# Combining merged into the next layer's mixer, block by block, in a two-layer mixer and MoE trunk on Trainium2

## The chip, the cores and the metric

The kernel runs on the 8 cores of one Trainium2 chip (two dies, cores 0 to 3 and 4 to 7). Each core works alone on half a sequence of a batch of four. The metric is the device time of the slowest core in microseconds.

## What is computed

```python
for l in range(DEPTH):                      # 2 layers, D_MODEL 1024, x is (4, 4096, 1024)
    m = hybrid_mixer(x, ...)                # z = x @ w_in (1024 x 2048); four groups of 256 channels:
    x = layer_norm(ALPHA * x + m, ln1)      #   spatial gating in chunks of 128, Conformer conv (31 taps),
    f = grouped_moe(x, ...)                 #   pooling over 2/4/8/16, gated conv (3 taps);
    x = layer_norm(ALPHA * x + f, ln2)      #   RMS norm of each group, then @ w_o (1024 x 1024)

def grouped_moe(x, ...):                    # 16 experts in 4 groups, best group, top 2 in it
    for e in range(N_EXPERTS):
        h = silu(xt @ w_gate[e]) * (xt @ w_up[e])              # 1024 x 512 each
        y = y + dense_gates[:, e:e + 1] * (h @ w_down[e])      # 512 x 1024
```

## The kernel before

A core holds 17 tiles of 128 tokens (2048 tokens and a halo tile) as f32 in `s_xtok`. MBLOCKS cuts them into block 0 (the halo) and blocks 1 to 4 (512 tokens each).

**Mixer.** For a block, `G_section` computes the spatial gating, `CPS_section` the other three groups, `O0_section` the product with w_o added to `s_xtok`, `A_section` the LN and a turned bf16 copy in `s_xT`, `R_section` the router; its `scatter` calls send each token's bf16 row to its two slots in `xg` in HBM (384 slots for an expert). The 31-tap convolution runs on PE as 62 matmuls for a block, each with a 128 x 128 diagonal `s_dg` that ACT or POOL makes just before, from `s_identf` and a column of taps, in four rotating buffers. RMS and LN over channels sum squares by f32 matmuls with `s_ones`.

**Experts.** `x_load` fetches an expert's 384 rows from `xg`, `x_turn` turns them, `s_wbuf` holds two experts' weights, and each result tile goes to `yg` in HBM. `cast_expert` has earlier copied the f32 weights (6.3 MB for an expert) to bf16 in HBM (`ew`), in two halves, on POOL's queue, with two in flight; `load_expert` reads them from there on SP's queue.

**Combining.** For each tile two gathers fetch the rows of its two experts from `yg`, DVE multiplies them by `geff` (the gates) and adds them to `s_xtok`; then LN, scale and shift (`s_lnp`), and for layer 1's input the turned copy. All 17 tiles pass before layer 1's mixer starts in earnest; the last stage does the same for 16 tiles and writes the output.

**Order.** A planner, `arrange`, orders each program stretch (layer 0 up to its experts, combining with layer 1, the last combining) by the longest chain behind each instruction, with a cost for each kind. Within an engine the order is then fixed, DMA issues too: an instruction that waits holds all behind it. A branch for overfull experts stands after each layer's experts and isn't taken.

At the start SP loads constants, parameters and x, then zeroes `xg` from `s_scrb`; POOL loads w_in and w_o as bf16. Helper lines of the profile: L549 matmul, L558 activation, L562 two-tensor, L569/L571 tensor-scalar, L577 scalar-tensor-tensor, L585/L587 copies on ACT/DVE, L621 LN statistics, L653 and L1196 transposes, L372 plain DMA, L375 scatter, L380 gather.

## Time and profile before

| | us |
|---|---|
| Median of 3 runs (2164.21 to 2168.35) | 2166.95 |
| The profiled execution, its own time | 2165.37 |
| Its span on the slowest core (core 1) | 2164.3 |
| PE busy (matmuls), ACT, DVE, POOL | 1319.7, 778.4, 954.6, 559.4 |
| The 8 cores' spans | 2128.2 to 2164.3 |

The span is from the first to the last instruction of core 1; the execution's own time is the slowest core's device time. Busy times overlap and say nothing alone; the stages have different limits and are read one by one.

### The profile page before, as it was taken

To read this page: it belongs to the slowest core of one execution; us is meant where nothing else is said; L and a number is where in the kernel's file an instruction comes from. 1 tells how busy PE (TensorE), PEld (TensorE's weight loads), DVE (VectorE), ACT (ScalarE), POOL (GpSimd) and SP (SyncE) were. 2 spreads that over 40 slices of the span, in tenths; PEclk is the share of its full clock that TensorE was granted. 3 is DMA by queue.
4 is the path that set the end of the run, shared out by engine and by line. 5 is a ranking of instruction groups with operands and counts; after the bars stand their busy time and mean duration, and the time that the engine had idled before them with its cause. 6 is when DMAs were issued, how large, how long until landed. Compare 5 with 4: busy or idle time off the path is not lost.

```text
span 2164.3 us, 26021 instructions; the slowest of 8 cores (2128.2 to 2164.3 us)
## 1 busy us (share of the span) xinstructions
PE 1319.7 (61%) x7130; PEld 644.5 (30%) x7130; DVE 954.6 (44%) x2121; ACT 778.4 (36%) x1478; POOL 559.4 (26%) x595
## 2 busy tenths in 40 slices
PE   3202858667576399999113475676757379999500
PEld 2101313223232255554101222222223145555200
DVE  0101563736447123333568453563727413323498
ACT  3202626446263222222224543545445322222022
POOL 3000305061334200000546403325152400000285
PEclk9655979879797599999555697888878689999855
DMA  9994599999993279996982799999999559998474
GB/s 207 232 141 121 59 119 105 108 136 109 125 144 129 103 265 315 323 306 226 195 209 93 99 111 107 114 110 135 109 149 123 169 187 306 317 318 301 184 235 165
DMA packets 85690, 379.22 MB, mean 175 GB/s; under 512 B 10528, under 2 KB 19488, under 8 KB 69664
## 3 DMA queue, kind: packets, MB, share of 16 engines
q0 software_dynamic: 31440, 165.59, 52.9%
q1 hardware_dynamic: 54096, 211.84, 29.5%
q8 instruction: 65, 1.06, 0.2%
q14 instruction: 89, 0.73, 0.1%
HBM read 402.47 MB, written 189.27 MB: 273 GB/s over the span
## 4 chain that ended last, share of the span: by engine, by line
PE 34%; DMA 34%; DVE 10%; issue 10%; another core or an unknown queue 5%; ACT 4%; POOL 2%; SPq 0%; DVEq 0%; ACTq 0%; POOLq 0%
PE pb L549 31%; DMA ew<-exp_w 28%; DMA s_scr<-yg,s_gai 2%; DVE s_xtok L577 2%; PE pT L1196 2%; DMA xg<-s_scrb,s_sci 1%; POOL s_xtok L562 1%; DMA s_scr<-gmwT 1%; DVE s_xtok L562 1%; DVE s_sm L621 1%; ACT s_xT L585 1%; DVE s_sm L577 1%; POOL xg L375 1%; DVE s_scr L562 1%
## 5 line engine op out<-in xcount | busy, mean ns | idle before, releaser
L549 PE MATMUL pb<-s_xT,s_wbuf 128*128 128x384 bf16 (+2 forms) x2992 | 677.6, 347 | 142.0 <-ACT s_scr L585 54.1
L549 PEld LDWEIGHTS pb<-s_xT,s_wbuf 128*128 128x128 bf16 x2992 | 279.0, 101 | 386.9 <-issue 215.9
L562 POOL TENSOR_TENSOR s_xtok<-s_xtok,s_lnp 128x1024 f32<-128x1024 f32 x99 | 246.3, 2507 | 85.0 <-ACT s_sm L558 42.8
L549 PE MATMUL pb<-s_hbb,s_dg 128*128 128x512 bf16 (+1 forms) x558 | 176.2, 400 | 141.1 <-POOL s_dg L571 77.0
L585 ACT COPY s_xT<-pT 128x1024 bf16<-128x1024 bf16 x163 | 164.7, 1010 | 229.6 <-PE pT L1196 205.5
L380 POOL DMA_INDIRECT s_scr<-yg,s_gai x46 | 62.7, 1364 | 652.1 <-DMA yg<-s_yT 611.3
L549 PE MATMUL pb<-s_wbuf,s_scrb 128*128 128x512 bf16 x768 | 221.3, 378 | 12.1 <-DVE s_xT L587 5.2
L653 PE MATMUL pT<-s_identb,s_scrb 128*128 128x128 bf16 x536 | 94.6, 261 | 176.7 <-ACT s_scrb L558 81.0
L372 POOL DMA_DIRECT2D ew<-exp_w x64 | 34.7, 543 | 597.4 <-DMA ew<-exp_w 531.6
L549 PE MATMUL pb<-s_wbuf,s_yT 128*128 128x512 bf16 x528 | 155.8, 417 | 34.9 <-DVE s_yT L577 30.3
L558 ACT ACTIVATE s_scr<-pb 128x384 f32<-128x384 f32 (+2 forms) x148 | 72.2, 499 | 266.0 <-PE pb L549 143.1
L558 ACT ACT_TABLE_LOAD x65 | 83.4, 1283 | 224.4 <-DMA xg<-s_scrb 82.5
L1196 PE MATMUL pT<-s_identb,s_xT 128*128 128x128 bf16 x768 | 133.8, 227 | 46.1 <-DMA s_xT<-xg 39.9
L562 DVE TENSOR_TENSOR s_scrb<-s_scr,pb 128x384 bf16<-128x384 f32 x128 | 68.5, 551 | 204.1 <-PE pb L549 165.5
L558 ACT ACTIVATE s_dg<-s_identf,s_ppb 128x128 bf16<-128x128 f32 x279 | 105.8, 397 | 125.9 <-PE pb L549 100.6
L571 POOL TENSOR_SCALAR s_dg<-s_identf,s_ppb 128x128 bf16<-128x128 f32 x279 | 108.2, 391 | 164.4 <-PE pb L549 122.3
L549 PEld LDWEIGHTS pb<-s_hbb,s_dg 128*128 128x128 bf16 x558 | 56.9, 103 | 227.6 <-issue 210.0
L558 ACT ACTIVATE s_scr<-s_scr 128x512 f32<-128x512 f32 (+1 forms) x144 | 85.5, 594 | 91.8 <-PE pb L549 29.9
L653 PEld LDWEIGHTS pT<-s_identb,s_scrb 128*128 128x128 bf16 x536 | 52.9, 117 | 205.9 <-issue 197.8
L587 DVE COPY s_xT<-pb 128x512 f32<-128x512 f32 x96 | 61.8, 686 | 116.8 <-PE pb L549 110.9
L587 DVE COPY s_yT<-pb 128x512 f32<-128x512 f32 x96 | 62.5, 686 | 112.5 <-PE pb L549 112.5
L549 PE MATMUL pb<-s_wbuf,s_xT 128*128 128x512 bf16 x264 | 104.0, 429 | 13.3 <-DMA s_wbuf<-w_in 11.2
(105 smaller groups left out, 1727.4 us busy)
## 6 DMA issues: line engine op xcount, KB each, us to landing
ew<-exp_w POOLq DMA_DIRECT2D x64, 1536.0 KB
s_wbuf<-ew SPq DMA_DIRECT2D x96, 1024.0 KB, 10.9
s_xT<-xg SPq DMA_DIRECT2D x32, 768.0 KB, 8.1
yg<-s_xT SPq DMA_DIRECT2D x48, 512.0 KB, 8.1
yg<-s_yT SPq DMA_DIRECT2D x48, 512.0 KB, 9.5
xg<-s_scrb SPq DMA_DIRECT2D x1, 12288.0 KB, 136.5
s_xtok<-x SPq DMA_DIRECT2D x17, 512.0 KB, 23.2
out<-s_xtok SPq DMA_DIRECT2D x16, 512.0 KB, 2.7
```

The costliest lines, as they stand in the source:

```text
L372: self._dma(E, lambda e: e.dma_start(out=out, in_=in_), semkey, w, r, group_left, size)
L375: self._dma(self.pool, lambda e: e.indirect_dma_start(out=out, out_offset=bass.IndirectOffsetOnAxis(ap=idx, axis=0), in_=in_, in_offset=None),
L380: self._dma(self.pool, lambda e: e.indirect_dma_start(out=out, out_offset=None, in_=in_, in_offset=bass.IndirectOffsetOnAxis(ap=idx, axis=0)),
L549: em.op(PE, lambda e: e.matmul(out.ap, lhsT.ap, rhs.ap, start=start, stop=stop), w=[out], r=[lhsT, rhs])
L558: em.op(ACT, lambda e: e.activation(out=out.ap, in_=in_.ap, func=func, **kw), w=[out], r=rr, tab={AF.Ln: "ln", AF.Exp: "ln", AF.Silu: "sil ...
L562: em.op(E, lambda e: e.tensor_tensor(out=out.ap, in0=a.ap, in1=b.ap, op=op), w=[out], r=[a, b])
L571: em.op(E, lambda e: e.tensor_scalar(out=out.ap, in0=a.ap, scalar1=a1, scalar2=a2, op0=op0, op1=op1), w=[out], r=rr)
L577: em.op(E, lambda e: e.scalar_tensor_tensor(out=out.ap, in0=a.ap, scalar=sv, in1=b.ap, op0=op0, op1=op1), w=[out], r=rr)
L585: em.op(E, lambda e: e.copy(out=out.ap, in_=in_.ap), w=[out], r=[in_])
L587: em.op(E, lambda e: e.tensor_copy(out=out.ap, in_=in_.ap), w=[out], r=[in_])
L653: em.op(PE, lambda e, kc=kc: e.transpose(out=pT(kc * 128, (kc + 1) * 128).ap, in_=xb(kc * 128, (kc + 1) * 128).ap, identity=identb().ap), ...
L1196: em.op(PE, lambda e_, src=src, dst=dst: e_.transpose(out=dst.ap, in_=src.ap, identity=identb().ap), w=[dst], r=[src, identb()])
```

## The change

Nine groups of edits, made together:

- Gates travel with the rows: `xg` rows are 1056 bf16 wide, with the f32 gate behind the 1024 values; the expert stage multiplies its output by the gate where DVE had copied it (half on DVE, half on ACT).
- Gathers add into `s_xtok` (`gather_add`); for a dropped token the index points to a zero row of `yg`. `C_section` (LN, scale, turned copy) takes the combining's place in layer 1's block loop, ahead of `G_section` of the same block.
- The 62 diagonals are made once a layer into `s_dgm`, by four POOL instructions in `load_layer_params`; layer 1's are made at the end of layer 0's mixer.
- Squares of two channel halves are added first, so one f32 matmul with `s_ones` stands where two stood.
- Only experts 0, 1 and the even ones (PRE) are cast to `ew`; 3, 5, ... 15 are loaded by POOL from the f32 weights into `s_wbuf`.
- Copies may run on ACT or DVE (AD) and sums on DVE or POOL (VP); the planner picks. Its DMA rate is 270 in place of 300 and its sizes for POOL's transfers are larger.
- At the start, `xg` is zeroed from `s_gov` in two halves of each row, after block 2's x tiles; blocks 3 and 4 of x come after it, casts after those. The identity arrives as bf16.
- `s_xT` (all blocks) and `s_yT` become one buffer `s_xy` with two blocks and yT; scratch shrinks.
- `dynamic_dma_scratch_size` is 4096 in place of 8192.

```diff
+PRE = [e for e in range(NE) if e % 2 == 0 or e == 1]
...
+        VP, AD = (DVE, POOL), (ACT, DVE)
...
+    def gather_add(self, out, in_, idx, semkey, w=(), r=(), group_left=0):
         self._dma(self.pool, lambda e: e.indirect_dma_start(
-            out=out, out_offset=None, in_=in_, in_offset=bass.IndirectOffsetOnAxis(ap=idx, axis=0)),
-            semkey, w, r, group_left)
...
             def sD(r, i):
-                tt(POOL, xtile(i), xtile(i), lnp(goff, goff + D), ALU.mult)
-                tt(POOL, xtile(i), xtile(i), lnp(goff + D, goff + 2 * D), ALU.add)
+                tt(VP, xtile(i), xtile(i), lnp(goff, goff + D), ALU.mult)
+                tt(VP, xtile(i), xtile(i), lnp(goff + D, goff + 2 * D), ALU.add)
...
         def rms_group(yf, nb, gcol, c0):
-            sq = S(TM0 + 2, 0, nb)
-            for j in range(2):
-                act(sq, yf[j], AF.Square)
-                mm(B[4](0, nb), ones(), sq, j == 0, j == 1)
+            sq, sq1 = S(TM0 + 2, 0, nb), S(TM0 + 1, 0, nb)
+            act(sq, yf[0], AF.Square)
+            act(sq1, yf[1], AF.Square)
+            vt(sq, sq, sq1, ALU.add)
+            mm(B[4](0, nb), ones(), sq, True, True)
             ve = S(TM0 + 1, 0, nb)
             ts(DVE, ve, B[4](0, nb), 1.0 / 256.0, ALU.mult, RMS_EPS, ALU.add)
             powm(ve, ve, nb)
...
+            for q in range(0, 62, 16):
+                m = min(16, 62 - q)
+                dst = dgm(q * 128, (q + m) * 128).v(lambda ap: ap.rearrange("p (k c) -> p k c", c=128))
+                idv = identb().v(lambda ap: ap.rearrange("p (o c) -> p o c", o=1).to_broadcast([128, m, 128]))
+                wv_ = ppb(PP_DW + q, PP_DW + q + m).v(
+                    lambda ap: ap.rearrange("p (k o) -> p k o", o=1).to_broadcast([128, m, 128]))
+                tt(POOL, dst, idv, wv_, ALU.mult)
...
+            if tag or e not in PRE:
+                for q in range(3):
+                    em.dma(POOL, wbuf(base + q * 4096, base + (q + 1) * 4096).ap, ew_d[l, e, :, q * 4096:(q + 1) * 4096],
+                           "dw%sp%d%s" % ("gud"[q], s, tag), w=[wbuf(base + q * 4096, base + (q + 1) * 4096)])
+                return
...
-        for b_ in range(2, len(MBLOCKS)):
-            x_in(b_, [wbuf(16384, 24576)])
-        em.dma(SP, xgD.ap[0:NSLOT, :].rearrange("(j p) d -> p j d", p=128),
-               scrb(0, D).ap.rearrange("p (o d) -> p o d", o=1).to_broadcast([128, NSLOT // 128, D]), "dz",
-               w=[xgD.rows(0, 1000)], r=[scrb(0, D), xtile(NT - 1)])
...
+        x_in(2, [wbuf(16384, 24576)])
+        for h in range(2):
+            em.dma(SP, xgD.ap[0:NSLOT, h * GW // 4:(h + 1) * GW // 4].rearrange("(j p) d -> p j d", p=128),
+                   gov(0, GW // 4).ap.rearrange("p (o d) -> p o d", o=1).to_broadcast([128, NSLOT // 128, GW // 4]), "dz",
+                   w=[xgD.rows(1000 * h, 1000 * h + 1000)], r=[gov(), xtile(8)], group_left=1 - h, size=NSLOT * GW)
+        x_in(3, [xgD.rows(0, 2000)])
+        x_in(4, [xgD.rows(0, 2000)])
+        for l in range(L):
...
+        for e in PRE:
+            cast_expert(0, e, [gtok.rows(NT - 1, NT)])
...
+        def c_gather(k, i, yg):
+            c = k * NT + i
+            em.gather_add(xtile(i).ap, yg.ap, gai(c, c + 1).ap, "dg%d" % (i + NT * k), w=[xtile(i), gtok.rows(i, i + 1)],
+                          r=[yg.rows(0, NSLOT + 1), gai(c, c + 1), xtile(i)])
...
-                            slot = dgi[0] % 4
-                            dgi[0] += 1
-                            wcol = ppb(PP_DW + j * 31 + k, PP_DW + j * 31 + k + 1)
-                            GE = (POOL, ACT, POOL, ACT)[slot]
-                            if GE is ACT:
-                                act(dg(slot * 128, (slot + 1) * 128), identf(), AF.Identity, scale=wcol)
-                            elif GE is DVE:
-                                ts(GE, dg(slot * 128, (slot + 1) * 128), identf(), wcol, ALU.mult)
-                            else:
-                                ts(GE, dg(slot * 128, (slot + 1) * 128), identf(), wcol, ALU.mult, 0.0, ALU.add)
-                            mm(pcs[j](0, nb), dg(slot * 128, (slot + 1) * 128), hbs[j](k, k + nb), k == 0, k == 30)
+                            q = (j * 31 + k) * 128
+                            mm(pcs[j](0, nb), dgm(q, q + 128), hbs[j](k, k + nb), k == 0, k == 30)
...
+                for k in range(2):
+                    xr, xf = xrow[b == nblk - 1], xrowf[b == nblk - 1]
+                    gcol = xf(0, nt * GW // 2).v(lambda ap: ap.rearrange("p (t c) -> p t c", t=nt)[:, :, D // 2:D // 2 + 1])
+                    gcol.box = xr[0](D, GW).box[:3] + (xr[nt - 1](D, GW).box[3],)
+                    cpy(DVE, gcol, ge.v(lambda ap: ap[:, k * nt:(k + 1) * nt].rearrange("p (t o) -> p t o", o=1)))
...
+                        em.scatter(xgD.ap, sci(c, c + 1).ap, xf(t * GW // 2, (t + 1) * GW // 2).ap, "dsc%d" % k,
+                                   w=[xgD.rows(c, c + 1), xgD.rows(1000 + c, 1001 + c)],
+                                   r=[xr[t](0, GW), sci(c, c + 1)], group_left=nt - 1 - t, size=128 * GW * 2)
...
+            def C_section(b):
+                t0, nb = MBLOCKS[b]
+                tiles = list(range(t0 // 128, (t0 + nb) // 128))
+                pipeline(tiles, ln_stages(2048) + xT_stages(scale0=hflag(), pt_fixed=0, rows=xbx))
+
+            if l > 0:
+                for (t0, nb) in MBLOCKS:
+                    for k in range(2):
+                        for i in range(t0 // 128, (t0 + nb) // 128):
+                            c_gather(k, i, ygD[l - 1])
+                for e_ in PRE:
+                    cast_expert(l, e_, [gtok.rows(NT - 1, NT)])
+            enter = X_section if l == 0 else C_section
+            enter(0)
             if skip0:
                 CPS_section(0)
             fb = 1 if skip0 else 0
+            if fb:
...
+                    enter(b + 1)
+                    G_section(b + 1)
+                    CPS_section(b + 1)
+                A_section(b)
+                R_section(b)
...
+            if not last:
+                load_layer_params(l + 1)
...
-                        cpy(DVE, yb(nh * 512, (nh + 1) * 512), pY())
+                        gate = gsl(s * CT + j, s * CT + j + 1)
+                        if nh == 0:
+                            ts(DVE, yb(nh * 512, (nh + 1) * 512), pY(), gate, ALU.mult)
+                        else:
+                            act(yb(nh * 512, (nh + 1) * 512), pY(), AF.Identity, scale=gate)
...
+        for g0 in range(1, NT, 4):
+            for k in range(2):
+                for i in range(g0, g0 + 4):
+                    c_gather(k, i, yg)
+        pipeline(list(range(1, NT)), ln_stages(2048) + [c_out])
```

The order of instructions at three places. First the start. SP before, from its first x tile to the first loads of cast weights:

```order
L372 DMA s_xtok<-x 128x1024
L372 DMA s_trash<-trash 128x34
L372 DMA s_ppb<-pp 128x86
L372 DMA s_bc<-bc 128x768
L372 DMA s_lnp<-lnp 128x2048
L372 DMA s_scr<-gmwT 128x512
L372 DMA s_xtok<-x 128x1024 x16
L372 DMA xg<-s_scrb 128x48x1024
L372 DMA s_wbuf<-ew 128x4096 x6
```

The same in the change:

```order
L402 DMA s_ebase<-ebase 128x16
L402 DMA s_trash<-trash 128x34
L402 DMA s_lnp<-lnp 128x2048
L402 DMA s_xtok<-x 128x1024 x4
L402 DMA xg<-s_gov 128x48x264 x2
L402 DMA s_xtok<-x 128x1024 x8
L402 DMA yg<-s_gov 4x1x256 x2
L402 DMA s_wbuf<-ew 128x4096 x4
L402 DMA s_ppb<-pp 128x86
```

The zeroing stood behind all 17 x tiles; now it stands behind nine, is in two parts and reads `s_gov`. DVE in the change, around its first write of `s_gov` (the router of block 0; `s_xtok<-s_xtok,pb` is the output sum of block 1's tiles):

```order
L629 COPY s_xy<-pT 128x8x128
L614 SCALAR_TENSOR_TENSOR s_scrb<-s_gtmp,s_sm,s_bc 128x256
L614 SCALAR_TENSOR_TENSOR s_xy<-s_scr,s_ppb 128x512 x2
L633 COPY s_scrb<-s_rb 128x1
L599 TENSOR_TENSOR s_gov<-s_rb 128x16
L614 SCALAR_TENSOR_TENSOR s_xtok<-s_xtok,pb 128x512 x2
L665 BN_STATS s_sm<-s_xtok 128x6 x2
L667 BN_AGGR s_sm<-s_sm 128x2
```

The write stands behind block 1's mixer and ahead of block 1's output sums. ACT before, around its first write into the part of `s_scrb` that the zeroing reads (the two `s_scrb<-s_scr,s_ppb 128x128`, of block 0's convolution):

```order
L558 ACTIVATE s_sm<-s_sm 128x1 x4
L585 COPY s_yT<-pT 128x256
L585 CAST s_scrb<-s_xtok 128x1024 x4
L585 COPY s_xT<-pT 128x8x128 x2
L558 ACTIVATE s_scrb<-s_scr,s_ppb 128x128 x2
L585 CAST s_scrb<-s_xtok 128x1024
L585 COPY s_scr<-pb 128x128
L585 COPY s_xT<-pT 128x8x128
L558 ACTIVATE s_scr<-s_scr 128x128
```

That write had the turned copies of block 1 around it. Second, POOL at the end of layer 0's mixer, before (`xg<-s_scrb,s_sci` are scatters):

```order
L571 TENSOR_SCALAR s_dg<-s_identf,s_ppb 128x128 x17
L372 DMA ew<-exp_w 48x16384
L375 DMA xg<-s_scrb,s_sci 10496x1024 x8
L562 TENSOR_TENSOR s_xtok<-s_xtok,s_lnp 128x1024 x8
L375 DMA xg<-s_scrb,s_sci 10496x1024 x8
L1243 TENSOR_LOAD s_flag
```

and in the change:

```order
L599 TENSOR_TENSOR s_xtok<-s_xtok,s_lnp 128x1024 x7
L405 DMA xg<-s_scrb,s_sci 10496x528 x4
L599 TENSOR_TENSOR s_dgm<-s_identb,s_ppb 128x2048
L405 DMA xg<-s_scrb,s_sci 10496x528 x4
L599 TENSOR_TENSOR s_dgm<-s_identb,s_ppb 128x2048
L405 DMA xg<-s_scr,s_sci 10496x528 x4
L599 TENSOR_TENSOR s_dgm<-s_identb,s_ppb 128x2048
L405 DMA xg<-s_scr,s_sci 10496x528 x4
L599 TENSOR_TENSOR s_dgm<-s_identb,s_ppb 128x1792
L402 DMA s_wbuf<-exp_w 128x4096 x21
L1318 TENSOR_LOAD s_flag
```

Layer 1's diagonals now stand between the scatters, and 21 loads of f32 expert weights follow. Third, POOL behind the branch, where combining begins, before:

```order
L380 DMA s_scr<-yg,s_gai 128x1024 x4
L380 DMA s_yT<-yg,s_gai 128x1024 x2
L372 DMA s_wbuf<-w_in 128x8x512
L380 DMA s_scr<-yg,s_gai 128x1024
L372 DMA s_wbuf<-w_in 128x8x256
L372 DMA s_wbuf<-w_in 128x8x768
L380 DMA s_scr<-yg,s_gai 128x1024
L372 DMA s_pwb<-cf_pw 128x2x256
L380 DMA s_scr<-yg,s_gai 128x1024
L372 DMA s_wbuf<-w_in 128x8x512
L380 DMA s_scr<-yg,s_gai 128x1024
L380 DMA s_yT<-yg,s_gai 128x1024
```

and in the change:

```order
L410 DMA s_xtok<-yg,s_gai 128x1024 x4
L402 DMA s_wbuf<-w_in 128x8x512
L410 DMA s_xtok<-yg,s_gai 128x1024 x3
L402 DMA s_wbuf<-w_in 128x8x256
L410 DMA s_xtok<-yg,s_gai 128x1024
L402 DMA s_wbuf<-w_in 128x8x768
L410 DMA s_xtok<-yg,s_gai 128x1024
L402 DMA s_wbuf<-w_in 128x8x512
L410 DMA s_xtok<-yg,s_gai 128x1024 x4
L402 DMA s_wbuf<-w_o 128x4x1024 x2
L410 DMA s_xtok<-yg,s_gai 128x1024 x9
L599 TENSOR_TENSOR s_xtok<-s_xtok,s_lnp 128x1024 x5
```

The gathers write `s_xtok` itself and stand nearly all ahead of the first pass with `s_lnp`.

## Rows read from the trace of the kernel before

**Rows 1.** The page: the span of the profiled execution.

```profile
span 2164.3 us, 26021 instructions; the slowest of 8 cores (2128.2 to 2164.3 us)
```

**Rows 2.** Stretches of core 1 by stage; under its header line.

```profile
core 1: us, PE busy (x) PEld busy (x) DVE busy (x) ACT busy (x) POOL busy (x), PEclk, DMA share, GB/s
0.00:205.00 205.00, 38.40 (x232) 23.99 (x232) 11.71 (x44) 43.02 (x88) 24.05 (x51) 0.67 0.94 185
205.00:735.00 530.00, 350.55 (x1617) 147.85 (x1617) 275.04 (x779) 258.99 (x527) 174.91 (x217) 0.83 0.80 111
735.00:1040.00 305.00, 283.05 (x1792) 157.50 (x1792) 94.87 (x164) 75.52 (x112) 0.00 (x0) 0.97 0.80 270
1040.00:1190.00 150.00, 32.83 (x173) 18.00 (x174) 104.79 (x145) 48.47 (x85) 89.77 (x56) 0.53 0.69 165
1190.00:1740.00 550.00, 332.59 (x1526) 139.97 (x1524) 265.59 (x703) 249.22 (x506) 181.82 (x224) 0.80 0.92 123
1740.00:2040.00 300.00, 282.29 (x1792) 157.13 (x1792) 94.47 (x160) 75.72 (x112) 0.00 (x0) 0.98 0.82 274
2040.00:2164.00 124.00, 0.00 (x0) 0.00 (x0) 108.10 (x128) 27.50 (x49) 88.83 (x48) 0.50 0.60 204
```

**Rows 3.** Waits from 0 to 210 us: waiter, awaited, us, times, longest.

```profile
ACT L558 <- DMA xg<-s_scrb: 82.5, 1, 82.5
```

**Rows 4.** DMA issues from 0 to 210 us: count, size, median us to landing.

```profile
xg<-s_scrb SPq DMA_DIRECT2D x1, 12288.0 KB, 136.5
```

**Rows 5.** Timeline of PE, start and length in us, at 93 us.

```profile
93.08 3.57 PE L549 MATMUL pb<-s_wbuf,s_xT 128*128 128x512 bf16 x8 [11.16 <-DMA s_wbuf<-w_in]
```

**Rows 6.** Groups of instructions, 205 to 735 us (layer 0 mixer).

```profile
L549 PE MATMUL pb<-s_hbb,s_dg 128*128 128x512 bf16 x248 | 80.7, 406 | 47.6 <-POOL s_dg L571 34.1 <-ACT s_dg L558 9.9 <-DVE s_hbb L577 1.4
L562 POOL TENSOR_TENSOR s_xtok<-s_xtok,s_lnp 128x1024 f32<-128x1024 f32 x34 | 79.6, 2359 | 28.1 <-ACT s_sm L558 25.1 <-ACT s_xtok L558 3.0
...
L549 PE MATMUL pb<-s_scr,s_ones 128*128 128x512 f32 (+1 forms) x88 | 47.5, 638 | 12.0 <-ACT s_scr L558 4.2 <-DVE s_rb L562 2.9 <-ACT s_sm L558 2.4
...
L558 ACT ACTIVATE s_dg<-s_identf,s_ppb 128x128 bf16<-128x128 f32 x122 | 45.8, 396 | 46.9 <-PE pb L549 44.8 <-PE pT L653 1.0
...
L558 ACT ACTIVATE s_xtok<-s_xtok,s_sm 128x1024 f32<-128x1024 f32 x17 | 20.9, 1236 | 16.3 <-DVE s_sm L577 16.3
```

**Rows 7.** The same, PE, 1190 to 1740 us (layer 1 mixer).

```profile
L549 PE MATMUL pb<-s_hbb,s_dg 128*128 128x512 bf16 x248 | 82.5, 427 | 83.0 <-POOL s_dg L571 40.5 <-ACT s_dg L558 19.8 <-DVE s_hbb L577 15.3
...
L549 PE MATMUL pb<-s_scr,s_ones 128*128 128x512 f32 x80 | 41.6, 616 | 10.4 <-ACT s_scr L558 4.7 <-ACT s_sm L558 3.7 <-DVE s_scr L562 1.5
```

**Rows 8.** Waits of POOL, 200 to 720 us.

```profile
POOL ew L372 <- DMA ew<-exp_w: 181.2, 19, 15.3
```

**Rows 9.** Waits of POOL, 1190 to 1700 us.

```profile
POOL ew L372 <- DMA ew<-exp_w: 258.2, 25, 21.8
```

**Rows 10.** DMA from 400 to 560 us (casts of expert weights).

```profile
DMA packets 1342, 19.10 MB, mean 119 GB/s; under 512 B 304, under 2 KB 304, under 8 KB 816
...
ew<-exp_w POOLq DMA_DIRECT2D x11, 1536.0 KB
```

**Rows 11.** DMA from 800 to 900 us (experts of layer 0).

```profile
DMA packets 7420, 31.93 MB, mean 319 GB/s; under 512 B 662, under 2 KB 662, under 8 KB 5294
...
q1 hardware_dynamic: 7412, 31.82, 97.2%
```

**Rows 12.** DMA rate in 40 slices of 1690 to 1740 us.

```profile
GB/s 426 416 426 423 439 410 357 321 233 105 16 0 13 0 0 0 177 308 341 13 0 0 0 0 0 0 0 0 0 0 39 210 213 213 213 216 213 213 148 20
```

**Rows 13.** DMA from 1040 to 1100 us (combining and weight loads).

```profile
DMA packets 7193, 12.44 MB, mean 207 GB/s; under 512 B 597, under 2 KB 4949, under 8 KB 7189
...
s_scr<-yg,s_gai POOLq DMA_INDIRECT x12, 21.2
```

**Rows 14.** Groups of instructions, 2040 to 2164 us.

```profile
L562 DVE TENSOR_TENSOR s_xtok<-s_xtok,s_lnp 128x1024 f32<-128x1024 f32 x16 | 37.5, 2345 | 5.3 <-POOL s_xtok L562 5.2
...
L380 POOL DMA_INDIRECT s_scr<-yg,s_gai x22 | 30.2, 1371 | 314.4 <-DMA yg<-s_yT 304.9 <-DVE s_sm L621 6.3 <-issue 2.5
```

396 lines of the change are left out of this document (198 added, 198 removed).

## The prediction

> **What bounds the kernel now.** I cut the span into stages first. The page gives the span, 2164.3 us, and the profiled execution's own time is 2165.4 us, which is 1.6 us under the median of the runs, 2166.95; I make the sum against 2165.4. [Rows 1, 2] Seven stretches tell different stories. Read per stretch how much of it PE, DVE, ACT and POOL fill, then the DMA share.
>
> From 0 to 205 us PE works 38 us. The list of waits names one event: ACT stands 82.5 us behind the DMA that zeroes xg, because ACT's next write goes into s_scrb, which that DMA reads. [Rows 3] The DMA takes 136.5 us. [Rows 4] Before it, PE waited for w_in until 93 us. [Rows 5]
>
> In the mixers (205 to 735, 1190 to 1740) no engine is full: PE 350 of 530 and 333 of 550 us, ACT and DVE about half. [Rows 2] The stages are chains over engines. Two groups stand out: the convolution's matmuls idle 47.6 us, 44.0 of it for their diagonals; in layer 1 they idle 83.0, 60.3 for them. [Rows 6, 7] POOL, which makes half of the diagonals, itself stands in its queue behind the casts of expert weights for 181 and 258 us. [Rows 8, 9]
>
> In the expert stages PE is nearly full, 283 of 305 and 282 of 300 us, and DMA is 97% busy as well. [Rows 2, 11] From 1040 to 1190 and 2040 to 2164 PE does next to nothing: this is the combining, run by DMA, DVE and POOL. [Rows 2]
>
> **The change part by part.**
>
> *Start.* The zeroing now reads s_gov and stands after five x tiles plus block 2's four; twelve of 17 x tiles come after the weights. Read side before the first full block: weights 12.6 MB in f32, five tiles 2.6, parameters and small tables 3.2, in all 18.4 MB. At 0.32 MB/us (below) that is 58 us, where PE had waited until 93 [rows 5]. From there to 205 us the kernel needed 112 us, 82.5 of them the stall [rows 3], so about 30: the state of 205 us is reached at 88 us at best, at 122.5 if only the stall goes. I take 100: **-105 us**. Where the stall goes: DVE's first write of s_gov must wait for the zeroing, and POOL's first scatter too. What is queued behind it is block 1's output sums, for which PE's output banks wait. The zeroing (13.0 MB in rows of 1056 bytes, half the old row) starts near 65 us and takes 41 us at 0.32, or 82 if the short rows cost double; it is over by 106 to 147. The s_gov write stands behind block 1's whole mixer, so near 150. I price the wait at nothing; cover gone, it is a rival. Casts start only after the last x tile, some 130 to 170 us. 18 halves at 160/11 = 14.5 us [rows 10] are 261 us, over by about 430, before the first expert. Hidden.
>
> *Mixer of layer 0 (530 us).* Diagonals are made once per layer, four POOL instructions of 2048 columns (by POOL's 2.36 us for 1024 [rows 6] 4.7 us each, 19 us, under the weight load). The 44.0 us of waits go, and ACT loses 45.8 us of work [rows 6], POOL about as much. The matmuls with s_ones in f32 halve: 47.5 / 2 = 24 us of PE [rows 6]. POOL's queue waits for fewer casts; its 181 us [rows 8] were mostly idle anyway, and I credit 15 us, for the LN passes and scatters behind them (bounds 0 and the 136 us that PE idles beside the diagonals). **-83 us**, to about 447. Copies that may go to ACT or DVE and sums that may go to DVE or POOL only smooth this; I credit nothing. The end of the mixer now has the next layer's diagonals between POOL's scatters: one instruction of 4.7 us stands ahead of the last four scatters. Small, inside my rounding.
>
> *Combining into the mixer (150 + 550 us).* Gates now multiply at the expert's output, where DVE copied anyway; half of these go to ACT, which is 75 of 305 us busy [rows 2]. Nothing. The 34 gathers add into s_xtok. Only block 0's and 1's ten gathers (5.2 MB) and w_in (8.4 MB read) stand before the mixer's first full block: 13.6 MB, 42 us at 0.325. If the adding reads and writes SBUF at a cost like a second transfer, ten times 1.6 us more, 58. I take 50, plus 30 for LN, turning and the first matmuls: 80 where 150 stood, -70. The mixer then loses 60.3 and 41.6 / 2 = 21 [rows 7], and gains the LN and turning of blocks 2 to 4: 12 tiles by some 3.3 us on ACT (the LN pass takes 1.24 [rows 6], and cast and copy are of its size), 40 us on an engine with 300 us free, and two passes of s_lnp each. I charge 16 us: -65. Together **-135 us**.
>
> The passes with s_lnp may now run on DVE. Beside POOL, DVE's takes 2.35 us for 1024 columns, as long as POOL's own in the mixer, so two passes at once gain nothing and I credit nothing for the free choice. [Rows 6, 14] The Trainium skill (SBUF — State Buffer, on the port pair that DVE and GpSimd share) says that a DVE instruction with two SBUF inputs and a GpSimd instruction that reads SBUF shut each other out for their whole length. The 2.35 us agrees; were the rule wrong, the passes of blocks 2 to 4 would halve and the sum be some 25 us less.
>
> *Experts.* Seven of 16 (3, 5, ... 15) are no longer cast to HBM and read back; POOL loads them as f32 into s_wbuf. For a pair of experts the HBM side moves 3.15 (cast one) + 6.29 (direct) + 1.58 (rows in) + 3.15 (rows out) = 14.2 MB, against 11.0. A pair has 35.7 us (305 and 300 us for 16 with their ends, of which 285 are matmuls). DMA is 97.2% busy at 319 GB/s already [rows 11]. What rate can it reach? Short bursts show 410 to 439 [rows 12]. Longest mixed stretches: the casts read 211 and write 105 GB/s (19.10 MB less 2.1 of eight scatters, over 160 us), with scatters 330 in all [rows 10]; 1040 to 1100 us wrote 12.44 MB and read 18.7 (the 6.3 MB of weights are f32 at the source), 312 GB/s [rows 13]. I take 325, the figure between, and nearest to the 319 of the stage itself: 14.2 / 0.325 = 43.5 us for a pair, 7.8 over PE's, by seven pairs 55 us for a layer, **+110 us** for two. Lower bound: at the bursts' 426, 33 us, hidden, 0. Upper: the direct load reads at the casts' 211 GB/s, 29.8 us in place of 7.4 (3.15 at 426) in the pair's 34.7: 57.1, +150 for a layer, +300. PE then waits for s_wbuf where today it waits for nothing.
>
> *Last stage (124 us).* DVE loses two sums of the gathers for a tile. It was DVE's and POOL's stage [rows 2]; now 32 gathers (16.8 MB) and the output (8.4 MB) are 77 us at 0.325, plus 18 for first landing and last tile: 95. POOL has 32 x 1.37 us of issues [rows 14] and some 15 passes, 79, under that. If adding doubles a gather, 147. I take 110: **-14 us**.
>
> Sum: 2165.4 - 105 - 83 - 135 + 110 - 14 = **1938 us**; about 1940 as a median.
>
> **Rivals.**
> 1. *Expert loads stay hidden.* For it: bursts of 426. Against: 97.2% busy at 319. 1938 - 110 = 1828 us. Chance 0.12.
> 2. *The memory side holds a middle rate*, half way between the casts' 330 and the lowest long burst, 410 [rows 10, 12]: 370 GB/s, 38.4 us for a pair, +19 for a layer instead of +55: 1866 us. For it: neither row is the mix to come. Against: no stretch of 50 us or more shows it. 0.12.
> The Trainium skill (HBM Reference, the bandwidth table) gives a core about 358 GB/s when both cores of a stack stream; by that alone a pair takes 39.5 us and the whole 1882. No stage here reaches it; the casts' 330 is nearest.
> 3. *Direct loads run at the casts' rate.* Same kind of transfer, though those write to HBM. 1938 + 190 = 2128 us. 0.10.
> 4. *Adding in the DMA costs a second transfer.* No row shows it. +8 at layer 1's start, +37 at the end: 1983 us. 0.13.
> 5. *The mixers don't get shorter* because dependent steps, not diagonals, set them, with smaller scratch and shared ports: the change doesn't do what it says. 83 + 65 back: 2086 us. For it: half-idle engines. Against: 104 us of waits by name [rows 6, 7]. 0.09.
> 6. *The zeroing is waited for again*, at s_gov, if it takes its 136 us from 65 on: DVE held until 200, +50: 1988 us. 0.07.
> 7. *Slower.* One mechanism: the f32 loads of seven experts starve PE. It decides when it costs 110 + 227 = 337 us, 24 for a pair, that is, when one direct load takes over 32.5 us; the casts' rate gives 29.8, so it needs them a tenth worse than anything here. 2200 us. 0.05.
> The forecast itself, within 45 us: 0.32.
>
> **The numbers.** The range 1825 to 2090 takes in cases 1, 2, 4, 5 and 6 and leaves out 3 and 7 and the far sides of the rest. Faster by over 0.2% (about what a measurement of this kernel can tell from no change) 0.93, the same 0.01, slower 0.06: every case but 7 ends below.
>
> **What would show it.** No 82 us wait of ACT near 100 us; block 1 underway at 100. No waits for diagonals; f32 matmuls with s_ones halved; experts of layer 0 starting near 550 us. Expert stages of some 355 us with PE waiting for s_wbuf from exp_w. Gathers landing at 6 us (one transfer) or 8 and more (two). The last stage at 110 us. Most fragile is the rate of the direct loads; next, how much of the mixers' idle time follows the diagonals.

## The result, and the profile after

The changed kernel takes 2118.99 us (median of 4 runs, 2117.39 to 2122.18) beside 2167.65 us for the kernel before on the same chip: ratio 0.978, 95% interval 0.9763 to 0.9797. I had forecast 1940 us, a gain of 225; 49 came, and the time lies above my range of 1825 to 2090. In some executions of these kernels one die or both ran at a lower granted clock and took longer (with eleven experts cast, below, 2056.62 us with four cores at 0.77 to 0.78, beside 2008.49 with all at 0.81 to 0.83); ratios and their intervals leave such executions out, the medians given do not.

The page's span, then the changed kernel's stretches under their header line, cut at the first read of rows of `xg`, the first gather, and, for layer 1, PE's first matmul of a full block.

```profile
span 2117.7 us, 23728 instructions; the slowest of 8 cores (2092.0 to 2117.7 us)
...
core 3: us, PE busy (x) PEld busy (x) DVE busy (x) ACT busy (x) POOL busy (x), PEclk, DMA share, GB/s
0.00:95.00 95.00, 33.15 (x240) 23.37 (x241) 24.48 (x81) 21.40 (x43) 23.83 (x22) 0.91 1.00 208
95.00:588.00 493.00, 321.63 (x1560) 140.44 (x1558) 325.19 (x837) 193.66 (x347) 145.20 (x106) 0.82 0.62 117
588.00:992.00 404.00, 311.73 (x1792) 162.53 (x1792) 96.34 (x172) 75.73 (x124) 12.58 (x22) 0.91 0.78 204
992.00:1100.00 108.00, 14.41 (x123) 11.14 (x124) 22.18 (x47) 22.12 (x39) 74.19 (x46) 0.53 1.06 198
1100.00:1605.00 505.00, 331.07 (x1535) 142.28 (x1533) 345.35 (x841) 202.60 (x365) 156.64 (x108) 0.79 0.44 94
1605.00:1995.00 390.00, 306.51 (x1792) 162.00 (x1792) 95.61 (x164) 75.30 (x124) 11.20 (x21) 0.92 0.79 211
1995.00:2118.00 123.00, 0.00 (x0) 0.00 (x0) 64.81 (x97) 27.04 (x49) 90.65 (x47) 0.50 0.88 205
```

Against [rows 2], by my own terms. In layer 1, PE's first matmul that streams the 512 tokens of a block (`pb<-s_xT,s_wbuf` 128x512 before, `pb<-s_xy,s_wbuf` after) stands 127 us behind the first gather before and 107 after, and the rest of that mixer fell from 571 to 506. The two traces' timelines give these; before, matmuls of single tiles begin already 74 us behind the first gather, after, at the same 107.

| term | forecast | came |
|---|---|---|
| start (state of 205 us reached) | -105 | -110 |
| mixer of layer 0 (530 to 493) | -83 | -38 |
| layer 1, first gather to first full block (127 to 107) | -70 | -20 |
| layer 1, the rest (571 to 506) | -65 | -65 |
| experts, layer 0 (305 to 404) and 1 (303 to 390) | +55, +55 | +99, +87 |
| last stage (123 to 123) | -14 | 0 |
| sum | -227 | -47 |

Two terms came as worked out. The experts are the largest miss, 76 us; the start of layer 1 (50) and the mixer of layer 0 (45) are the next, then the last stage (14).

The groups that answer to [rows 6, 14]: the convolution and ones matmuls, POOL's passes with `s_lnp` in the mixer of layer 0; then gathers and passes of the last stage.

```profile
L599 POOL TENSOR_TENSOR s_xtok<-s_xtok,s_lnp 128x1024 f32<-128x1024 f32 x27 | 65.8, 2437 | 78.4 <-ACT s_xtok L595 65.5 <-DVE s_xtok L599 6.4 <-DVE s_rb L599 5.0
L586 PE MATMUL pb<-s_hbb,s_dgm 128*128 128x512 bf16 x248 | 54.8, 379 | 0.8 <-DVE s_scrb L633 0.7
...
L586 PE MATMUL pb<-s_scr,s_ones 128*128 128x512 f32 x40 | 27.6, 779 | 12.4 <-POOL s_scr L624 10.6 <-DVE s_rb L599 1.9
...
L410 POOL DMA_INDIRECT s_xtok<-yg,s_gai x32 | 54.4, 1700 | 58.9 <-DMA yg<-s_scr 51.0 <-issue 7.5 <-DMA s_xtok<-yg,s_gai 0.3
L599 POOL TENSOR_TENSOR s_xtok<-s_xtok,s_lnp 128x1024 f32<-128x1024 f32 x15 | 39.1, 2603 | 18.8 <-ACT s_sm L595 15.4 <-ACT s_xtok L595 2.7
L599 DVE TENSOR_TENSOR s_xtok<-s_xtok,s_lnp 128x1024 f32<-128x1024 f32 x17 | 29.0, 1707 | 15.0 <-POOL s_xtok L599 7.8 <-ACT s_xtok L595 6.5 <-ACT s_sm L595 0.3
```

The 47.6 us of idle time at the convolution are 0.8, and the ones matmuls fell by 20 us. Yet the mixer lost only 38: as a reader of a profile I would count 67 us gone by name.

PE's and ACT's waits in the experts of layer 0, 610 to 980 us, and one row of ACT's timeline there:

```profile
PE pb L586 <- ACT s_scr L595: 22.0, 25, 2.6
PE pb L586 <- DMA s_wbuf<-exp_w: 19.9, 7, 4.0
PE pT L1264 <- DMA s_xy<-xg: 12.7, 3, 11.4
...
ACT s_scr L595 <- DMA yg<-s_scr: 53.0, 11, 11.4
...
760.41 0.97 ACT L595 ACTIVATE s_scr<-pb 128x384 f32<-128x384 f32 x2 [8.62 <-DMA yg<-s_scr]
```

The 128x384 activation is the silu, not the output; all eleven of these waits of ACT stand before such a one. Why should a silu wait until an output tile has been written to HBM? Because of where its buffer lies. The silu goes to `SG(k, CAP)`, `s_scr` columns 542 k to 542 k + 384; the output buffers now lie in `s_scr` from 768 on, where before they had `s_xT` and `s_yT`. The second silu buffer, 542 to 926, overlaps the first output buffer.

Layer 1's start, ACT's timeline and then POOL's:

```profile
1058.82 1.04 ACT L631 CAST s_scr<-s_xtok 128x1024 bf16<-128x1024 f32 x1 [26.64 <-POOL s_xtok L599]
...
1036.58 1.68 POOL L410 DMA_INDIRECT s_xtok<-yg,s_gai  x1 [0.27 <-issue]
...
1052.33 1.55 POOL L410 DMA_INDIRECT s_xtok<-yg,s_gai  x1 [0.27 <-issue]
1053.32 7.72 POOL L599 TENSOR_TENSOR s_xtok<-s_xtok,s_lnp 128x1024 f32<-128x1024 f32 x3
...
1075.67 1.55 POOL L410 DMA_INDIRECT s_xtok<-yg,s_gai  x1
...
1091.25 2.95 POOL L599 TENSOR_TENSOR s_xtok<-s_xtok,s_lnp 128x1024 f32<-128x1024 f32 x1
```

POOL's passes for the first blocks stand behind two rows of gathers of later blocks, 1036 to 1053 and 1075 to 1091 us. ACT and PE wait for these passes: the turned copies of block 1 can't be made before them.

### The profile page after: what moved, and what is told of

It is laid out like the page before. It is cut to its first block, busy times and chain, and to the rows that moved or that the text cites. A ratio compares the mean times of both kernels' runs of the same rounds, so it can differ in the third digit from the quotient of the medians.

```text
span 2117.7 us, 23728 instructions; the slowest of 8 cores (2092.0 to 2117.7 us)
## 1 busy us (share of the span) xinstructions
PE 1318.5 (62%) x7040; PEld 641.8 (30%) x7040; DVE 974.0 (46%) x2238; ACT 617.9 (29%) x1089; POOL 514.3 (24%) x370
## 3 DMA queue, kind: packets, MB, share of 16 engines
q1 hardware_dynamic: 54080, 168.23, 23.7%
## 4 chain that ended last, share of the span: by engine, by line
PE 36%; DMA 20%; issue 17%; DVE 15%; POOL 6%; ACT 5%; DVEq 0%; another core or an unknown queue 0%; ACTq 0%; SPq 0%; POOLq 0%
PE pb L586 34%; DMA yg<-s_scr 13%; DMA s_xy<-xg 4%; POOL s_xtok L410 3%; ACT s_scr L595 2%; DMA s_xtok<-yg,s_gai 2%; DVE s_scr L599 2%; DVE s_rb L599 1%; POOL s_xtok L599 1%; PE pT L1264 1%; DVE s_scrb L614 1%; ACT L595 1%; DVE s_sm L614 1%; DVE s_sm L665 1%; DVE s_scr L606 1%
## 5 line engine op out<-in xcount | busy, mean ns | idle before, releaser
L586 PE MATMUL pb<-s_xy,s_wbuf 128*128 128x384 bf16 (+2 forms) x2992 | 741.9, 364 | 206.1 <-ACT s_scr L595 66.9
L586 PEld LDWEIGHTS pb<-s_xy,s_wbuf 128*128 128x128 bf16 x2992 | 289.8, 104 | 510.5 <-issue 349.1
L586 PE MATMUL pb<-s_wbuf,s_xy 128*128 128x512 bf16 x792 | 247.9, 423 | 13.5 <-DVE s_xtok L614 5.0
L1264 PE MATMUL pT<-s_identb,s_xy 128*128 128x128 bf16 x768 | 117.4, 234 | 87.2 <-DMA s_xy<-xg 79.0
L629 DVE COPY s_xy<-pT 128x1024 bf16<-128x1024 bf16 (+1 forms) x124 | 80.7, 651 | 148.2 <-PE pb L586 53.8
L410 POOL DMA_INDIRECT s_xtok<-yg,s_gai x66 | 109.5, 1660 | 122.2 <-DMA yg<-s_scr 102.3
L586 PE MATMUL pb<-s_hbb,s_dgm 128*128 128x512 bf16 (+1 forms) x558 | 116.5, 370 | 26.8 <-POOL s_dgm L599 22.9
L586 PEld LDWEIGHTS pb<-s_wbuf,s_xy 128*128 128x128 bf16 x792 | 81.6, 106 | 126.1 <-issue 65.0
L665 DVE BATCH_NORM_STATS2 s_sm<-s_xtok 128x6 f32<-128x512 f32 x132 | 85.9, 681 | 62.3 <-DMA s_xtok<-yg,s_gai 61.2
L595 ACT ACTIVATE s_xtok<-s_xtok,s_sm 128x1024 f32<-128x1024 f32 x66 | 81.3, 1238 | 79.8 <-DVE s_sm L614 67.5
```

Of the source, the lines that this page charges most:

```text
L410: self._dma(self.pool, lambda e: e.indirect_dma_start(out=out, out_offset=None, in_=in_, in_offset=bass.IndirectOffsetOnAxis(ap=idx, axis= ...
L586: em.op(PE, lambda e: e.matmul(out.ap, lhsT.ap, rhs.ap, start=start, stop=stop), w=[out], r=[lhsT, rhs])
L595: em.op(ACT, lambda e: e.activation(out=out.ap, in_=in_.ap, func=func, **kw), w=[out], r=rr, tab={AF.Ln: "ln", AF.Exp: "ln", AF.Silu: "sil ...
L629: em.op(E, lambda e: (e.copy if e is ACT.e else e.tensor_copy)(out=out.ap, in_=in_.ap), w=[out], r=[in_])
L665: em.op(DVE, lambda e, c=c: e.bn_stats(out=SMT(i, c * 6, c * 6 + 6).ap, in_=xtile(i, c * 512, (c + 1) * 512).ap), w=[SMT(i, c * 6, c * 6 + ...
L1264: em.op(PE, lambda e_, src=src, dst=dst: e_.transpose(out=dst.ap, in_=src.ap, identity=identb().ap), w=[dst], r=[src, identb()])
```

## The experiments

Ratios are to the kernel before on the same chip, with 95% intervals; stages are of the profiled execution's slowest core, "start" being layer 0's first read of rows. The changed kernel: 0.978, start 588, experts 404 and 390. Where the experts load directly, their stage is not the same on all cores of one execution: in the changed kernel layer 0's takes 389 to 404 us on the eight cores, 398 at the mean, and layer 1's 390 to 397. So 10 us in the expert stage of one core say little, and I give the mean of the eight where it matters.

**What the direct loads cost alone.** In the kernel before, seven experts of a layer are loaded directly and no longer cast; the rest of its work stays. The branch that does it:

```diff
+            if not tag and e not in PRE:
+                for q in range(3):
+                    em.dma(POOL, wbuf(...).ap, ew_d[l, e, :, q * 4096:(q + 1) * 4096], ...)
+                return
```

> The kernel before with one part of the change: experts 3, 5, ... 15 loaded directly as f32 by POOL, nine cast. Theory A: expert stages from 305 and 300 us to 390 to 410 us each, here too; the mixers, whose POOL queue stood 181 and 258 us behind the casts, shorten by 15 to 40 us each: total 2270 to 2330 us. Rival B (output path): expert stages stay near 305 us, total 2090 to 2150 us.

2204.02 us, 1.0115 (1.0091 to 1.014). Experts take 356 and 362 us, +51 and +59. The DMA of 710 to 1040 us:

```profile
DMA packets 17794, 77.82 MB, mean 236 GB/s; under 512 B 1575, under 2 KB 1575, under 8 KB 12394
...
q1 hardware_dynamic: 14746, 55.49, 49.3%
q0 software_dynamic: 3024, 22.02, 43.5%
```

The software queue's 22.02 MB are bf16 on arrival and twice that at the source: 99.8 MB in 330 us, 303 GB/s. My term of +55 a layer was right. The mixers meanwhile gained, from fewer casts alone: the start is at 698 and not 736, and from the first gather to layer 1's experts it takes 671 us and not 698. The stretch of layer 0's mixer, to set beside 530 us in [rows 2], and POOL's waits for casts, 200 to 690 us, beside 181.2 in [rows 8]:

```profile
205.00:698.00 493.00, 345.69 (x1620) 146.37 (x1618) 273.65 (x781) 259.53 (x530) 168.56 (x203) 0.85 0.46 75
...
POOL ew L373 <- DMA ew<-exp_w: 93.2, 9, 15.2
```

This is the length that the changed kernel's mixer has, 493 us, with the diagonals still made just before use. In the kernel before, the chain that ended last runs through the casts' transfers for 42.1% of layer 0's mixer and 70.9% of layer 1's; here it is 3.7% of layer 0's.

**The overlap of silu and output buffers.**

```diff
-                    sg = SG(fc % 2, CAP)
+                    sg = scr((fc % 2) * CAP, (fc % 2 + 1) * CAP)
```

> The changed kernel with one line other: the silu buffers of the expert stage at columns 0 and 384 of s_scr, not 0 and 542, so that the second (542 to 926) no longer overlaps the first output buffer (768 to 1792). Theory C (this overlap makes the silu of every other chunk wait until an output tile has landed in HBM, and the output tile wait for the silu's readers): the waits of ACT for yg, 53 us in 610 to 980 us, go; an expert takes 21.5 us as in the kernel before with direct loads, instead of 24.7; both expert stages shorten by 40 to 50 us; total 2020 to 2050 us. Rival A alone (only the direct loads' bytes hold the stage): same time, 2110 to 2125 us.

2066.27 us, 0.9473 (0.9445 to 0.9502): a one-line edit gains three points, more than the whole change had gained. Experts 371 and 369. ACT's and PE's waits, 610 to 950 us:

```profile
ACT s_scr L595 <- DMA yg<-s_scr: 31.7, 4, 15.8
...
PE pb L586 <- DMA s_wbuf<-ew: 19.7, 3, 12.5
PE pb L586 <- DVE s_xy L629: 9.2, 8, 1.7
PE pb L586 <- ACT s_scr L595: 8.5, 9, 1.9
```

PE now waits for weights, as I had expected of the change. ACT's four waits left are those of output tiles. At the mean of the eight cores the stages fell from 398 and 393 us to 366 and 365.

**The gates at the expert's output**, all on DVE, none on ACT.

```diff
-                        if nh == 0:
+                        if True:
                             ts(DVE, yb(nh ...
```

> The changed kernel with the gate of both output halves applied by DVE, none by ACT. Theory D (the ACT half of the output delays the silus queued behind it): expert stages shorten by 20 to 40 us each, 2040 to 2080 us. Theory C (overlap of buffers, whoever writes): within 15 us of the changed kernel, 2105 to 2135 us, the stall only sits on DVE instead.

2144.26 us, 0.9827 (0.9797 to 0.9857), experts 419 and 408. From 610 to 980 us ACT still waited 62.2 us for output writes, each time with a silu. So ACT's share of the gates was not the cause.

**Adding in the gathers.** The second row then replaces, and nothing is summed.

```diff
-            out=out, out_offset=None, in_=in_, in_offset=bass.IndirectOffsetOnAxis(ap=idx, axis=0),
-            compute_op=ALU.add), semkey, w, r, group_left)
+            out=out, out_offset=None, in_=in_, in_offset=bass.IndirectOffsetOnAxis(ap=idx, axis=0)),
+            semkey, w, r, group_left)
```

> The changed kernel with gathers that overwrite the rows of s_xtok instead of adding to them (the sum of the residual and the two experts is left out; all else is the same). If adding costs a second transfer, the landing of a gather falls by 1.5 us and more, the last stage from 112 to about 75 us and the combining of layer 0 by 20 to 40 us: 2040 to 2065 us. If adding is free: the same time as the changed kernel, 2110 to 2125 us.

2096.08 us, 0.9615 (0.9586 to 0.9644). From first gather to layer 1's experts 591 us, not 613; last stage 106, not 123. The last stage's gathers and DMA, without the adding:

```profile
L410 POOL DMA_INDIRECT s_xtok<-yg,s_gai x32 | 33.2, 1037 | 56.8 <-DMA yg<-s_scr 47.9 <-issue 7.6 <-DMA s_xtok<-yg,s_gai 0.9
...
q0 software_dynamic: 4608, 16.78, 49.1%
```

and with it, in the changed kernel:

```profile
q0 software_dynamic: 4608, 16.78, 70.0%
```

For the same 16.78 MB, adding holds the DMA engines for 70.0% of 123 us, 86, in place of 49.1% of 105, 52: 1.7 times as long. POOL's issue is 1.70 us in place of 1.04. The two places where it adds are 22 and 17 us shorter without. The slowest core's span fell by only 20, since its experts took 411 and 399; at the mean of the eight cores they take 398 and 396, as in the changed kernel, and the span falls by 32. This core is one with long expert stages.

**The second gate**, that is copied into the rows before their second scatter, left out (both scatters carry the first).

```diff
-                    cpy(DVE, gcol, ge.v(
+                    if k == 0:
+                      cpy(DVE, gcol, ge.v(
```

> The changed kernel without writing the gate of the second expert into the rows (those rows travel with the first expert's gate; the output is wrong by that). If the second set of scatters waits for the first to land because the gate column is rewritten (7.4 us at the end of layer 0's mixer, and within the blocks), each mixer's end shortens by 5 to 10 us: 2100 to 2112 us. If it is hidden: 2115 to 2122 us.

2110.32 us, 0.9664 (0.9602 to 0.9726); start at 577. That is 11 us in layer 0's mixer, at whose end, in the changed kernel, the second scatters wait 7.4 us for the first to land. From the first gather to layer 1's experts it is 603 us, 10 fewer, or 589 in place of 607 at the mean of the cores. So this copy costs 10 to 20 us in each mixer, a term that my sum did not have.

**The start alone.** In the kernel before, only the source of the zeroing was moved, to columns of `s_xT` that are free then.

```diff
-               scrb(0, D).ap.rearrange("p (o d) -> p o d", o=1)
+               zs.ap.rearrange("p (o d) -> p o d", o=1)
```

> The kernel before, with the rows that zero xg read from a stretch of s_xT that is free at that time; nothing else is changed. My sum priced ACT's stall of 82.5 us and the order of loads together at -105. If the stall alone is worth its length, the first mixer ends about 80 us sooner (experts of layer 0 at 655 us where they start at 736) and the time is 2085 to 2095. If another wait takes its place (the casts end at 629, the first scatter waits for the zeroing, the weights come late), less: 2110 to 2165.

2115.38 us, 0.9719 (0.968 to 0.9759): this alone gains at least as much as the whole change (2.8 points and 2.2). Start at 678, 58 sooner. POOL's waits, 200 to 670 us, show what stands now where the other 24 of the 82.5 us may have gone:

```profile
POOL xg L375 <- DMA xg<-s_xT: 62.9, 1, 62.9
```

The first scatter now waits for the zeroing, which takes 144.2 us beside seven casts. In the changed kernel no cast runs beside it: its two parts are issued at 76 us and have landed at 121, and nothing waits for them.

**Do waits for diagonals hold the mixers?** From both sides: sixteen buffers in the kernel before (with the DMA scratch at 4096, as in the changed one), and diagonals made again for each block in the changed one.

```diff
-        dg = sb("dg", 4 * 128, BF16)
+        dg = sb("dg", 16 * 128, BF16)
```

> The kernel before with sixteen buffers for diagonals in place of four. My sum took the convolution's waits for diagonals, 44.0 us in layer 0's mixer and 60.3 in layer 1's, as time on the path: most of it goes here, and the time falls by 60 to 100 us (2075 to 2115). If these waits lie beside other chains, as keeping the diagonals showed in the changed kernel, the waits shrink and the time stays within 10 us.

2162.16 us, 0.9923 (0.9898 to 0.9948). The waits fell less than I expected; the convolution's matmuls in the two mixers:

```profile
L549 PE MATMUL pb<-s_hbb,s_dg 128*128 128x512 bf16 x242 | 60.3, 396 | 40.0 <-POOL s_dg L571 37.0 <-DVE s_sm L577 2.3 <-DVE s_hbb L577 0.5
...
L549 PE MATMUL pb<-s_hbb,s_dg 128*128 128x512 bf16 x240 | 66.5, 431 | 63.3 <-POOL s_dg L571 22.3 <-ACT s_dg L558 20.8 <-DVE s_hbb L577 19.5
```

27 us of idle time went against [rows 6, 7], 22 of them waits for diagonals, and 17 us of the time (0.77%): more than the 10 of the one theory, far less than the 60 to 100 of the other. The busy time of these matmuls fell too, by 36 us, as they now stand closer together (six and eight of 248 are missing from the records). So some 60 us went from these rows and 17 from the kernel.

```diff
-            for q in range(0, 62, 16):
-                ...
-                tt(POOL, dst, idv, wv_, ALU.mult)
...
+                            if slot % 2:
+                                act(dgm(q, q + 128), identb(), AF.Identity, scale=wcol)
+                            else:
+                                ts(POOL, dgm(q, q + 128), identb(), wcol, ALU.mult, 0.0, ALU.add)
```

> The changed kernel with the diagonals made for each block by ACT and POOL in four rotating slots, as before the change, all else the same. If keeping the diagonals is worth what its waits and matmuls show (47 + 26 us in layer 0, 80 + 25 us in layer 1), the time rises by 100 to 180 us, 2220 to 2300 us. If the mixers are set by DVE's and the block chain's other steps, it rises by under 60 us, 2120 to 2180 us.

2118.85 us, 0.9714 (0.9678 to 0.975). ACT works 43 us more from 95 to 660 us; from 130 to 580 PE idles 10.8 us before the convolution's matmuls, 5.0 of it for POOL's diagonals; and the start is at 584. Kept diagonals are worth nothing in this kernel.

**Does PE hold the mixers?** Silu buffers apart, and 23 of the convolution's 31 taps left out.

```diff
-                    for k in range(31):
+                    for k in range(8):
```

> The changed kernel, silu buffers apart, with eight of the convolution's 31 taps (23 are left out). PE loses 4 blocks x 46 matmuls x 0.379 = 70 us of a mixer, and block 0's. If PE's row of work holds the mixer, each gets 60 to 75 us shorter and the time is near 1930. If steps over DVE, ACT and POOL hold it, each gets shorter by less than 30: 2010 to 2060.

2018.85 us, 0.9292 (0.9255 to 0.9329); start 573, layer 1's gathers to experts 586 where it was 605 with all taps. From 95 to 573 us:

```profile
95.00:573.00 478.00, 279.69 (x1337) 121.36 (x1360) 323.75 (x843) 189.19 (x345) 139.58 (x101) 0.78 0.73 121
```

With all taps PE was busy 325.02 us from 95 to 588. It lost over 40 us of work, though at a granted clock of 0.78 in place of 0.81, and the mixer lost 15. PE does not hold it.

**Does DVE, by the free choice of engines?** Every free copy on ACT, every free sum on POOL.

```diff
-        VP, AD = (DVE, POOL), (ACT, DVE)
+        VP, AD = POOL, ACT
```

> The changed kernel, with every copy that may run on ACT or DVE put on ACT, and every sum that may run on DVE or POOL put on POOL, as before. If DVE's added work (330 us busy of 502 in the first mixer, where it had 275 of 530) is what holds the mixers, they get shorter by 15 to 40 us each and the time falls to 2040 to 2090. If the free choice does what it is for, the time rises, by 10 to 60 us. If the chain is one of dependent steps on any engine, it stays within 10 us of the changed kernel.

2184.92 us, 1.0056 (1.0025 to 1.0086), all that the change had gained is gone: the free choice, which I priced at nothing, is worth some 60 us. Start 599 (+11), gathers to layer 1's experts 628 (+15), last stage 137 (+14), experts 413 and 402 (+9, +12). DVE is busy 296.87 us in the first mixer in place of 325.19, and the mixer is longer, so my suspicion of DVE's added work falls. The last stage shows what the choice saves there. On fixed engines, its stretch, its groups (2042 to 2178 us), and one row of DVE's and of POOL's timeline:

```profile
2042.00:2178.00 136.00, 0.00 (x0) 0.00 (x0) 66.50 (x80) 27.56 (x49) 123.80 (x64) 0.50 0.84 185
...
L599 POOL TENSOR_TENSOR s_xtok<-s_xtok,s_lnp 128x1024 f32<-128x1024 f32 x32 | 81.8, 2819 | 3.1 <-ACT s_xtok L595 3.1
...
L614 DVE SCALAR_TENSOR_TENSOR s_sm<-s_sm 128x1 f32<-128x1 f32 x16 | 40.4, 2523 | 11.8 <-ACT s_sm L595 11.8
...
2157.39 5.50 DVE L614 SCALAR_TENSOR_TENSOR s_sm<-s_sm 128x1 f32<-128x1 f32 x1 [0.69 <-ACT s_sm L595]
...
2155.35 7.51 POOL L599 TENSOR_TENSOR s_xtok<-s_xtok,s_lnp 128x1024 f32<-128x1024 f32 x3
```

Two things are to be seen. POOL is full: 123.80 of 136 us, where it is 90.65 of 123 with the free choice, and between its passes it waits 3.1 us in place of 18.8. And a DVE instruction of a single column takes 2.5 us at the mean, in place of 0.7 with the free choice (x16, 11.5 us): the one shown ends with POOL's three passes. As POOL waits only 3.1 us for what comes of such steps, they don't lengthen this stage; POOL's own work does.

Why does DVE relieve POOL, when a DVE pass with `s_lnp` takes as long as POOL's [rows 14]? Two passes on DVE, the first in the kernel before, beside a pass of POOL, the second in the changed kernel:

```profile
2099.00 3.24 DVE L562 TENSOR_TENSOR s_xtok<-s_xtok,s_lnp 128x1024 f32<-128x1024 f32 x1
...
1022.51 1.22 DVE L599 TENSOR_TENSOR s_xtok<-s_xtok,s_lnp 128x1024 f32<-128x1024 f32 x1
```

The 2345 ns of [rows 14] are a mean over two kinds: seven of these 16 passes take 1.2 us and nine 3.2. Alone, DVE's pass takes half as long as POOL's, which never takes under 2.3. With the free choice 11 of the last stage's 17 passes on DVE take 1.2 us.

**Does the smaller scratch?** Silu buffers apart, diagonals for each block, and in their room a buffer of its own for the third convolution's input.

```diff
+        chx = sb("chx", 2 * 544)
-                chls = [(lambda a, c, j=j: S(CH0 + j, a, c)) for j in range(2)]
+                chls = [(lambda a, c, j=j: chx(j * 544 + a, j * 544 + c)) for j in range(2)]
```

> The changed kernel with the silu buffers apart, and in the room of the kept diagonals (made for each block again, four buffers) a buffer of its own for the third convolution's input, which shares s_scr with the pooling section's. If the smaller scratch of the mixers holds them, each mixer is 15 to 40 us shorter than with the silu buffers apart alone: ratio 0.91 to 0.935. If it does not: 0.94 to 0.95, as that kernel.

2055.97 us, 0.945 (0.9417 to 0.9483): as with the silu buffers apart alone. That shared buffer is not it.

**Do the casts?** Silu buffers apart, and all sixteen experts direct.

```diff
-PRE = [e for e in range(NE) if e % 2 == 0 or e == 1]
+PRE = []
```

> The changed kernel, silu buffers apart, without casts: all sixteen experts of a layer are loaded direct. If the casts beside it hold the mixer, layer 0's experts start at 550 us or sooner where they start at 588; if they are hidden, within 8 us of 588. A layer's experts, 303 us with none direct, 337 with four and 371 with seven, take about 303 + 16 x 9.5 = 455 us if each direct load costs the same; by 6.29 + 2.37 + 0.79 MB for an expert at 320 GB/s 29 us each, 470. In all some 2230.

2150.24 us, 0.9891 (0.9841 to 0.9941). Start 569, 19 sooner; gathers to layer 1's experts 593, 12 fewer. Experts 439 and 427: +8 us for each direct load, over the 303 us that a layer takes in the kernel before, with none. My expectation had counted 0.79 MB of an expert twice: its load and rows are 8.65 MB, which in 439 / 16 = 27.4 us is 315 GB/s.

**How many casts, and at what pace.** First the changed kernel with sixteen and with twelve experts cast, at the planner's 17.5 us for a half expert.

```diff
+PRE = list(range(NE))
```

> The changed kernel with all 16 experts cast to HBM (PRE is the list of all), no direct f32 load. Theory A (the seven direct f32 loads lengthen the expert stages, from 305 and 300 us to 410 and 400): both expert stages fall back to 300 to 320 us; the casts, 32 halves by 14.5 us from about 140 us on, end near 600 us, so the mixers grow by 20 to 60 us for both layers together; total 1960 to 2000 us. Rival B (it is the new output path, the gate on ACT and the landing of yg, 15 us instead of 8 to 10, that holds PE): the expert stages stay near 400 us and the total at 2120 to 2180 us.

2312.85 us, 1.0617 (1.0583 to 1.0651). Casts run to 737 us and, in layer 1, to 1813, and the experts wait for them: start 663, and 430 us of experts. Since this kernel's casts begin at 178 us, behind the last x tile, and before's at 59, there is no room for 32 halves.

```diff
+PRE = [e for e in range(NE) if e % 4 != 3]
```

> The changed kernel with 12 of 16 experts cast (all but 3, 7, 11, 15), four direct. Theory A: each direct load costs about 105/7 = 15 us where the neighbours can't absorb it, so the expert stages take at most 60 us more than with none, 305 to 360 us; if a direct load every fourth expert can be spread over four slots, nearly nothing, and the total is at or below that of all cast, 1950 to 2010 us. Rival B: stages near 400 us, 2110 to 2140 us.

2153.96 us, 0.988 (0.9839 to 0.9921): experts 378 and 378, but start 640. Then with the silu buffers apart:

> The changed kernel with the silu buffers apart and twelve experts cast, at the planner's own pace. Experts of a layer 337 us as in the run with the denser pace. If the number of casts holds the start of the experts, it is at 640 to 655 us and 1640 again, and the time 2065 to 2090; if only the dense pace did, 590 and 1570, and 2010.

2064.2 us, 0.9473 (0.944 to 0.9506): experts 334 and 332, start 643, layer 1's at 1610. The experts gain 74 us, and the mixers lose it. With a denser plan:

```diff
-... size=64 * 12288 * 6)
+... size=64 * 12288 * 4)
-def arrange(ops, hop=0.12, dma_gbs=270.0):
+def arrange(ops, hop=0.12, dma_gbs=300.0):
```

> The changed kernel with the silu buffers apart, twelve experts cast in place of nine, and a planner that puts the casts at 10.5 us for a half in place of 17.5. If four direct loads for a layer cost what the seven do each (a seventh of some 65 us), a layer's experts take 340 us, and with casts done before the experts start (24 halves of 14.5 us from 180 us: 530) nothing is lost ahead: 2066 less 2 x 30 = 2005 us, ratio 0.92. If the casts then hold POOL's queue or the loads, the experts start later than 590 and 1565 us by up to 50 each: 2060 to 2110.

2087.78 us, 0.9581 (0.9532 to 0.963): experts 342 and 328, start 653. Both starts are late for reasons of POOL's queue, but not for the same one. POOL's waits of the dense plan, 160 to 640 us, and then, at the planner's own pace, POOL's timeline at the end of the mixer:

```profile
POOL ew L402 <- DMA ew<-exp_w: 163.9, 17, 14.8
```

```profile
593.31 0.54 POOL L402 DMA_DIRECT2D ew<-exp_w  x1 [7.85 <-DMA ew<-exp_w]
597.96 1.02 POOL L405 DMA_INDIRECT xg<-s_scr,s_sci  x1 [4.11 <-DVE s_sci L599]
...
611.20 0.57 POOL L402 DMA_DIRECT2D ew<-exp_w  x1 [8.40 <-DMA ew<-exp_w]
631.61 1.01 POOL L405 DMA_INDIRECT xg<-s_scr,s_sci  x1 [19.84 <-DVE s_scr L633]
```

A cast takes 14.3 to 14.5 us back to back. Planned at 10.5, POOL waits for the cast before and all its sums stand behind it; at 17.5, where it waits 23.7 us for casts, the last casts fall between the last scatters. So a pace between them, with twelve and with eleven cast:

```diff
-... size=64 * 12288 * 6)
+... size=int(64 * 12288 * 5.3))
```

> Silu buffers apart, twelve experts cast, each half planned at 15.5 us: over the 14.3 us that a half takes at back to back, under the 17.5 at which the last casts fall between the last scatters. If POOL's waits for casts are what costs, experts start near 600 and take 335 us, in both layers: 2066 less 2 x 34 plus 12 is 2010, ratio 0.925. If twelve casts cost the mixer by their number, experts start at 640 and 1610 again: 2060.

2006.87 us, 0.927 (0.9245 to 0.9295), beside 2165.87: experts 332 and 328, start 622, layer 1's at 1556.

> The same with eleven experts cast, each half at 16.4 us. Where POOL's waits are the cost: start near 592, experts 345 us, 2066 less 2 x 25 is 2015. Else 2050 to 2060.

2013.39 us, 0.929 (0.9262 to 0.9318), at `5.6` and without expert 13's casts: start 615, experts 344 and 337. Both came as forecast in total. The start, 622 and not 600, did not: one cast still stands ahead of the last scatters. The number of casts costs something too, as the kernel without them had shown. Twelve casts at this pace is the fastest version found.

## Why the prediction was wrong

The time left the range because four terms of the sum fell short, all to the same side: the experts by 76 us, layer 1's start by 50, layer 0's mixer by 45, the last stage by 14. The free choice of engines, priced at nothing, was worth some 60 the other way and hides part of it.

**Start: right.** -105 forecast, -110 came; no wait at `s_gov` from the zeroing, which is over at 121 us, inside the forecast 106 to 147. So rival 6 falls.

**Experts: the step that failed most.** "7.8 over PE's, by seven pairs 55 us" holds: +51 and +59 measured alone. The rest stands in the sentence "Gates now multiply at the expert's output ... Nothing". I costed the multiplies and not the place to which they write. The output buffers' move into `s_scr`, on top of a silu buffer, costs 33 and 21 us of the 99 and 87 (404 to 371, 390 to 369) and 60 us of the profiled span. The remaining 15 and 7 us of the stages (10 and 12 at the mean of the cores), against 356 and 362 in the kernel before with direct loads, stay open. Neither kernel without the adding or without gates on ACT has shorter expert stages, but both still had the overlap. Rivals 1, 2, 3 and 7, on the direct loads' rate, fall.

**Layer 1's start: -20 for -70.** I had let the first full block come 42 to 58 us after the first gather and took 50, plus 30 for LN, as though the passes ran on arrival. They stand in POOL's queue behind gathers that they don't need, 1.55 us of issue each, 9 at a time. The prediction counts these issues for the last stage and not here. The Trainium skill (PSUM — Partial Sum Buffer, Engine vs sequencer instructions) calls GpSimd's queue strict FIFO; the timeline's 26.64 us agree. The adding itself is part of it: without it PE's first full block begins 92 us after the first gather, not 107. No run moved the gathers behind the passes, so how much of the other 35 us is their place in the queue is read from the timeline and not shown.

**Rival 4 (adding costs a second transfer) came in part:** 1.7 times a plain gather's DMA time, 39 us in the two places where I had priced +45. I had it at 0.13 since no row showed it. In the last stage my 110 lay between 95 us without and 147 with a second transfer; the runs gave 106 and 123.

**Mixers: the sum came in layer 1 and half of it in layer 0, and the steps are wrong in both.** The terms "the 44.0 us of waits go" and "24 us of PE" are true as rows and not as time, and "I credit 15 us" for POOL's fewer casts was too little. Shown: fewer casts alone give 38 us in layer 0's mixer of the kernel before, all that the change gained there, and 27 in layer 1. In the kernel before, 22 us fewer waits for diagonals gave 17; in the changed one, more than 40 us less of PE's work gave 15, diagonals made for each block again cost nothing, the shared buffer tried costs nothing, the other casts cost 19 and the copy of the second gate 11. That is rival 5's mechanism, at 0.09, in part: the mixers did get shorter, but not by what keeping the diagonals and halving the f32 matmuls took away; each of these lies for the most part beside another chain. The -65 of layer 1 is then luck: a sum that came right while its parts (fewer casts give 27, fixed engines take back 15) are not those that I named. Which steps make up the 490 us that remain is not settled: none of the edits to the changed kernel shortens layer 0's mixer by more than 19.

**Free choice of engines: 60 us for "I credit nothing".** I argued from DVE's 2.35 us that two passes at once gain nothing. The step that failed is the reading of that row: its mean holds passes of 1.2 us and passes of 3.2 that wait for POOL's. The Trainium skill (SBUF — State Buffer, Who interferes with whom) has the shared port pair as an exclusive lock, and 3.24 us beside a pass of POOL and 1.22 otherwise agree. So two passes don't run at once, and yet a pass on DVE holds the pair half as long as one on POOL, whose queue was full. The single-column steps of LN show the same lock, 2523 ns for one column at the mean on fixed engines and 719 with the choice. The last stage's 14 us are explained by POOL's work; no run splits the 26 in the mixers and the 21 in the experts.

## What to carry to other kernels

When a change moves a buffer, check every user of its new columns, and price a place as you price an instruction: the overlap here cost more than the change had gained. A wait's length in a stage where no engine is full is an upper bound: here between nothing and three quarters of it came back, so ask which chain ends last (before, it ran through the casts) and price that one. A mean of a group of instructions can hold two kinds, alone and waiting: look at single ones. And on an in-order queue that issues transfers and computes, count the issues that stand ahead of each pass, and plan transfers at the pace at which they land: here a quarter too dense blocked the queue, and a fifth too sparse ran into the last scatters.

## What the runs showed of the hardware that I had not expected

- A gather that adds into SBUF holds the DMA engines 1.7 times as long as a plain one (86 and 52 us for 16.78 MB) and POOL's issue takes 1.70 us in place of 1.04.
- The zeroing of `xg`: one DMA of 12288 KB took 136.5 us beside casts [rows 4] and 144.2 with its source moved; two of 6336 KB, in rows half as long and without casts beside them, took 44 us together, about the 41 that I had forecast. No run tells the casts' part from that of the rows' length.
- Direct loads cost 6 to 10 us each with four, seven or sixteen in a layer: nearly linear.
- A DVE pass over 128x1024 f32 takes 1.2 us alone and 3.2 beside a pass of POOL, which takes 2.3 at the least. A one-column DVE instruction, 0.14 us alone, took 2.5 at the mean beside POOL's passes on fixed engines.
